# Delta rule: triangle inverses doubled by 64x64 array tiles, with the next pair's levels between this pair's state products

## What is computed

```python
lower = where(strict, einsum('bhntd,bhnsd->bhnts', k_beta, k) * decay, 0)
unit_lower = lower + eye(c)
u = triangular_solve(unit_lower, v_beta)
w = triangular_solve(unit_lower, k_beta * exp(g)[..., None])
attn = where(tri, einsum('bhntd,bhnsd->bhnts', q, k) * decay, 0)
k_tail = k * exp(g_last - g);  q_dec = q * exp(g)
# over the chunks:
v_new = u - w @ state
o = q_dec @ state + attn @ v_new
state = exp(g_last) * state + k_tail.T @ v_new
```

## Time and profile before

| what | value |
|---|---|
| runs | 1901.27, 1905.84, 1907.29 us; median 1905.84 |
| span of the profiled execution | 1897.2 us; of the execution that was profiled the page gives the span alone |
| the median run less that span | 8.6 us |
| the stage: first turn of keys (L1185) to its last output (L1160) | 351.5 to 432.1 us of the span |
| u and w of the four pairs begin at | 365.66, 383.58, 403.35, 422.30 us |
| busiest engine of the whole program | PE, 94% of the span |

### The profile page before, as it was taken

One profiled execution on the slowest core, in us unless ns is written; L12 is line 12 of the kernel. 1 busy time (PEld: TensorE's weight loads), 2 busy tenths in 40 slices (PEclk: granted clock), 3 DMA queues, 4 the chain that ended last, 5 costly groups with the idle time before them and its releaser, 6 DMA issues. The chain is left out here.

```text
span 1897.2 us, 20762 instructions
## 1 busy us (share of the span) xinstructions
PE 1779.8 (94%) x8544; PEld 941.4 (50%) x8544; DVE 697.1 (37%) x1423; ACT 405.5 (21%) x721; POOL 66.4 (3%) x61
## 2 busy tenths in 40 slices
PE   7999999998999998999999999988799999999885
PEld 6785445794555554555543444434355434434342
DVE  3558774453334334444322222212423222222124
ACT  2421332442321222231111111111111111111111
POOL 0000000610000000210000000000000000000000
PEclk9999999999999999999999999999899999999998
DMA  5343332008499992835799999999796999999995
GB/s 211 134 165 135 133 134 49 1 1 356 175 416 412 412 413 106 298 150 219 328 427 429 429 429 429 429 429 427 277 426 276 429 429 428 429 428 430 429 426 220
DMA packets 74531, 583.48 MB, mean 308 GB/s; under 512 B 19323, under 2 KB 21499, under 8 KB 31421
## 3 DMA queue, kind: packets, MB, share of 16 engines
q1 hardware_dynamic: 69677, 580.43, 74.1%
q10 hardware_dynamic: 4752, 1.61, 0.3%
HBM read 578.83 MB, written 3.15 MB: 307 GB/s over the span
## 5 line engine op out<-in xcount | busy, mean ns | idle before, releaser
L1850 PE MATMUL gate_ps_l<-pool,hT 128*64 128x512 f32 x576 | 151.7, 593 | 11.0 <-DMA pool<-in_expert_w_gate 5.7
L1850 PE MATMUL up_ps_l<-pool,hT 128*64 128x512 f32 x576 | 141.7, 595 | 9.2 <-DMA pool<-in_expert_w_up 7.9
L1876 PE MATMUL y_ps_l<-pool,hidden_l 128*64 128x512 f32 x576 | 145.4, 595 | 4.2 <-DMA pool<-in_expert_w_down 2.7
L393 PE MATMUL proj_ps<-pool,hT 128*128 128x512 f32 x320 | 138.3, 592 | 0.0
L2016 DVE SCALAR_TENSOR_TENSOR y_low_l<-y_ps_l,slot_gate_l,y_high_l 128x512 fp32r<-128x512 f32 x64 | 47.9, 751 | 193.5 <-ACT y_high_l L1957 193.5
L385 PE MATMUL proj_ps<-hT,pool 128*128 128x256 f32 x512 | 113.6, 384 | 0.0
L385 PEld LDWEIGHTS proj_ps<-hT,pool 128*128 128x128 f32 x512 | 98.1, 192 | 15.3 <-issue 1.8
L2006 DVE TENSOR_TENSOR hidden_l<-hidden_l,up_ps_l 128x512 f32<-128x512 f32 x32 | 22.0, 688 | 215.3 <-PE up_ps_l L1850 215.3
L393 PEld LDWEIGHTS proj_ps<-pool,hT 128*128 128x128 f32 x320 | 60.8, 190 | 74.4 <-issue 74.1
L1850 PEld LDWEIGHTS gate_ps_l<-pool,hT 128*64 128x64 f32 x576 | 49.8, 137 | 94.7 <-issue 94.7
L1850 PEld LDWEIGHTS up_ps_l<-pool,hT 128*64 128x64 f32 x576 | 45.6, 137 | 85.4 <-issue 85.4
(11 more groups left out here) (534 smaller groups left out, 2896.1 us busy)
## 6 DMA issues: line engine op xcount, KB each, us to landing
pool<-in_expert_w_up SPq DMA_DIRECT2D x36, 2048.0 KB, 30.2
pool<-in_expert_w_down SPq DMA_DIRECT2D x36, 2048.0 KB, 29.7
pool<-in_expert_w_gate SPq DMA_DIRECT2D x36, 2048.0 KB, 31.1
pool<-in_w_in_blocks SPq DMA_DIRECT2D x18, 2048.0 KB, 7.5
gate_room<-in_expert_w_gate SPq DMA_DIRECT2D x14, 2048.0 KB, 24.9
store<-in_expert_w_up SPq DMA_DIRECT2D x14, 2048.0 KB, 22.3
pool<-in_moe_w_gate SPq DMA_DIRECT2D x12, 2048.0 KB, 12.7
pool<-in_moe_w_up SPq DMA_DIRECT2D x12, 2048.0 KB, 12.1
```

Of the source, the lines that this page charges most:

```text
L393: last = mm(pp[:, n % 2, j * W:(j + 1) * W], k.hT[:, c, j * P:(j + 1) * P], wbuf[n % 2][:, c, :], start=(c == 0), stop=(c == KC - 1))
L1850: last = mm(out[e * CAP:(e + 1) * CAP, 0:H], xg(part * r + c)[:, 0, at:at + CAP], ex.weights(i, e, c), start=(part + c == 0), stop=(part = ...
L1876: last = mm(Y[e * CAP:(e + 1) * CAP, n], hidT[:, part * r + c, e * CAP:(e + 1) * CAP], ex.weights(i, e, c)[:, n * W:(n + 1) * W], start=(p ...
```

## The change

- The inner level (32 to 64) is done within the two 64x64 halves of a 128x128 tile: rows 0..63 and 64..127 separately, each a 64x64x64 product. `HALF` names the halves. The upper half's product reads partitions 0..63 and writes 0..63, the lower half's 64..127 and 64..127; calls alternate between them.
- X transposed back is no longer made by turning: the half that the outer level needs is computed directly as `zt` beside `z` (L1248 and L1251 of the new kernel).
- The outer level (64 to 128) computes only the one 64x64 block that is not zero: 4 products for `nL · XT` and 4 for the update. No mask is needed; ACT copies the first result out (`outer_out`) and writes the second straight into XT (`outer_inverse`), which POOL has set to zero once.
- POOL spreads over two block columns instead of four: 256 elements per matrix instead of 512.
- The levels of pair `it + 1` stand between the state products of pair `it`, in new PSUM banks `L[a]` (`gdn_level_ps`); `B` becomes `M1`, `M2` (`gdn_u_ps`, `gdn_w_ps`). Before the loop the levels of pair 0 run alone.
- The scaling of head 1's keys and values moves from ACT (12 instructions) to DVE (3 instructions of 512 elements). ACT's sums of squares move behind the second scaling and write into `k.ob`. q · state is written to `M2` and counted by the same semaphore as w · state; the scaled value goes to a buffer of its own (`qs`).

Only tables and this stage differ. In the constant tables `lev` shrinks from 512 to 128 columns and `same_block` from 128 to 64.

Its core:

```diff
-        X2, XT2, kbg2, ktl2, vb2 = (sb(full, 2) for _ in range(5))
-        V, us, wT = (sb(full) for _ in range(3))
-        B = [[k.ps(f"gdn_ps{a}_{b}", full) for b in range(3)] for a in A]
+        full, square = [P, 2, NJ, P], [P, 2, NJ, CH]
+        kbg2, ktl2, vb2 = (sb(full, 2) for _ in range(3))
+        X2, XT2 = (sb(square, 2) for _ in range(2))
+        XT, us, wT = (sb(full) for _ in range(3))
+        V0 = sb(square)
+        V1, X1 = (sb([P, NJ, CH]) for _ in range(2))
+        S, vn, qs = (sb([P, 2, P]) for _ in range(3))
+        L = [k.ps(f"gdn_level_ps{a}", [P, 2, 2 * NJ * CH]) for a in A]
+        M1, M2 = ([k.ps(f"gdn_{n}_ps{a}", full) for a in A] for n in ("u", "w"))
...
+                for a in A:
+                    nc.gpsimd.memset(XT[a][:], 0.0).then_inc(s_zero[a], 1)
...
+                def outer_out(it):
+                    for a in A:
+                        act.wait_ge(s_v1[a], it + 1)
+                        nc.scalar.activation(V1[a][:], by_tile(L[a][:, 0]), ACT.Copy).then_inc(s_v1s[a], 1)
+
+                def outer_inverse(it):
+                    for a in A:
+                        act.wait_ge(s_z1[a], it + 1)
+                        for d in range(2):
+                            nc.scalar.activation(XT[a][HALF[d], d, :, HALF[1 - d]], by_tile(L[a][HALF[d], 1]),
+                                                 ACT.Copy).then_inc(s_x1[a], 1)
...
+                def inner_inverse(it):
+                    for a in A:
+                        dve.wait_ge(s_z0[a], it + 1)
+                        dve.wait_ge(s_zero[a], 1)
+                        z = by_unit(L[a][:, 1])
+                        for d, r in enumerate(HALF):
+                            tt(X1[a][r], X2[it % 2][a][r, d], by_tile(L[a][r, 0]), ALU.add).then_inc(s_x0[a], 1)
+                            tt(XT[a][r, :, :, r], XT2[it % 2][a][r], z[r], ALU.add).then_inc(s_x0[a], 1)
...
+                def inner(it):
+                    for a, h in heads(it):
+                        pe.wait_ge(s_id[a], 2 * it + 2)
+                        if it:
+                            pe.wait_ge(s_x1[a], 2 * it)
+                        v = by_unit(L[a][:, 0])
+                        for d, j in units():
+                            for r in HALF:
+                                last = mm(v[r, d, j], k.nL[r, h, d, j, r], XT2[it % 2][a][r, d, j],
+                                          start=True, stop=True)
+                        last.then_inc(s_v0[a], 1)
+
+                def inner_update(it):
+                    for a in A:
+                        pe.wait_ge(s_v0s[a], it + 1)
+                        z, zt = by_unit(L[a][:, 1]), by_tile(L[a][:, 0])
+                        X = X2[it % 2][a]
+                        for j in range(NJ):
+                            for d, r in enumerate(HALF):
+                                mm(zt[r, j], V0[a][r, d, j], X[r, d, j], start=True, stop=True)
+                        for d, j in units():
+                            for r in HALF:
+                                last = mm(z[r, d, j], X[r, d, j], V0[a][r, d, j], start=True, stop=True)
+                        last.then_inc(s_z0[a], 1)
+
+                def outer(it):
+                    for a, h in heads(it):
+                        pe.wait_ge(s_x0[a], 4 * it + 4)
+                        v = by_tile(L[a][:, 0])
+                        for j in range(NJ):
+                            for d in range(2):
+                                to, of = HALF[d], HALF[1 - d]
+                                last = mm(v[to, j], k.nL[of, h, d, j, to], XT[a][of, d, j, of], start=True, stop=True)
+                        last.then_inc(s_v1[a], 1)
```

More of the change, by code:

```diff
@@ L81, in tables @@
     )
[L82 to L89, removed]
+    half = (p >> L0) & 1
+    inside, across = np.arange(CH)[None, :] >> L0, np.arange(2 * BS)[None, :] >> L0
+    out["lev"] = np.concatenate([f((half == 0) & (inside == 1)), f((half == 1) & (inside == 0))], 1)
+    out["same_block"] = f(half == across)
     r = np.arange(BS * BS)
@@ L1080, in scaled @@
                 def scaled(it):
[L1081 to L1086, removed]
-                scaled(0)
@@ L1089, in _ @@
[L1089 to L1094, removed]
-                for it in range(NI):
[L1096 to L1102, removed]
+                    act.wait_ge(s_turned[0], it + 1)
@@ new lines, in outer_inverse, with squares @@
+                def outer_inverse(it):
[4 more added lines that the diff above has]
+                                                 ACT.Copy).then_inc(s_x1[a], 1)
+                def squares():
+                    for j in range(NJ):
+                        for h in range(GLA_H):
+                            out = (k.ob[:, j, (h + 1) * GLA_DV:(h + 2) * GLA_DV] if h + 1 < GLA_H
+                                   else squared[:, j])
+                            nc.scalar.activation(out, k.oa[:, j, h * GLA_DV:(h + 1) * GLA_DV], ACT.Square,
+                                                 accum_out=k.mix_var[:, j, h:h + 1]).then_inc(k.s_mix_sq, 1)
@@ L1171, in _ @@
             def _(pe):
-                def each(fn):
-                    for d, j in units():
-                        last = fn(d, j)
-                    return last
                 mm, turn, ident = nc.tensor.matmul, nc.tensor.transpose, k.table("ident")
@@ L1188, in _, with outer_update @@
+                def outer_update(it):
+                    for a in A:
+                        pe.wait_ge(s_v1s[a], it + 1)
+                        z = by_tile(L[a][:, 1])
+                        for j in range(NJ):
+                            for r in HALF:
+                                last = mm(z[r, j], X1[a][r, j], V1[a][r, j], start=True, stop=True)
+                        last.then_inc(s_z1[a], 1)
                 turned(0)
+                inner(0)
+                inner_update(0)
@@ new lines, in _ @@
+                    more = it + 1 < NI
+                    for a in A:
+                        pe.wait_ge(s_nb[a], (12, 3)[a] * (it + 1))
+                        pe.wait_ge(s_x1[a], 2 * it + 2)
+                        if it:
+                            pe.wait_ge(s_hd[a], it)
+                        for d, j in units():
+                            mm(M1[a][:, d, j], XT[a][:, d, j], vb[a][:, d, j], start=True, stop=True)
+                        for d, j in units():
+                            last = mm(M2[a][:, d, j], kbg[a][:, d, j], XT[a][:, d, j], start=True, stop=True)
+                        last.then_inc(s_uw[a], 1)
@@ L1216, in _ @@
+                    if more:
                         turned(it + 1)
+                        inner(it + 1)
                     for a, h in heads(it):
-                        aT = k.aT[:, h]
                         pe.wait_ge(s_uws[a], 2 * it + 2)
                         for d in range(2):
-                            j = first(d)
-                            last = mm(B[a][2][:, 0, d], ktl[a][:, d, j], us[a][:, d, j], start=True, stop=True)
+                            last = mm(M2[a][:, 0, d], ktl[a][:, d, d], us[a][:, d, d], start=True, stop=True)
```

160 lines of the change are left out of this document (86 added, 74 removed).

## The result

The changed kernel takes 1886.89 us (median of 6 executions, 1878.06 to 1890.78), the kernel before 1903.13 beside it (6 executions); the ratio is 0.9919, 95% interval 0.989 to 0.9948. In two later comparisons the same kernel gave 1882.36 against 1900.81 (0.9905) and 1885.43 against 1902.55 (0.9924). The forecast was 1889.4.

The account below looks back on a forecast made before the run. PE was taken to bound the stage. Rounds -14.6, start -3.8 and clock +2.0 sum to -16.4 us off the median 1905.84: 1889.4 us; own range 1884 to 1895, 8 in 10 within 1883 to 1902.

Parts of the forecast that it names:

- The total: Whole kernel: -16.4 us off the median of 1905.84, giving 1889.4 us.
- A small pass at 0.028 us: PE, 64x64 products of the levels: two tiles run side by side, 0.028 us per pass, ends 0.028 and 0.111.
- PE's sum: PE's work per round: 8.9 us full passes, 3.1 small passes, 1.05 changes of shape, together 13.1 us.
- The change of shape: PE switching between full and small tiles: 0.15 us towards small, 0.20 back, three each way, 1.05 us per round.
- The round of 14.0: One pair's u and w to the next's: DVE's tail ends it at 14.0 us; three rounds give -14.6 us.
- The start: Stage start up to the first u and w: these begin at 361.85 instead of 365.66, -3.8 us.
- The clock: PE around the first u and w: 1.2 GHz lasts 3 to 7 us longer, costing +2.0 us.
- The last piece: Stretch after the three rounds, without levels: 9.7 to 9.9 us, no change.
- The first, one tile at a time: Rival 1, PE's small passes: 0.055 us each, rounds 16.5 including 0.35 of waits, kernel 1898.7 us; chance 0.23.
- The second: Rival 2, PE's instruction pace: small passes cost 0.111 us, rounds 22.6, kernel slower at 1918.2 us; chance 0.10.
- 0.062 us per pass: Skill's floor per matmul where firmware decodes, named under rival 2: round 17.4 us, kernel near 1901.
- The third: Rival 3, clock falls inside the rounds through small tiles and gaps: about 3 us per round, kernel 1898; chance 0.12.

Follow-up runs that it names:

- the second profile: The kernel before, unchanged, profiled once more: stage 79.8 us, starting at 357.5 instead of 351.5, rounds 17.92, 19.77 and 18.95 us.
- The split: Two kernels against the kernel before: small tiles with levels ahead of their own u and w, 1899.75 us (1.000); the change's order with full products, 1901.45 us (1.0002).

## Why the prediction held, and where not

**The total** held, 1889.4 against 1886.89, a difference of -16.2 us where -16.4 was summed. That it came so close is luck in part. In the stage the sum promised -16.4, and the profiles show -13.8 (80.6 to 66.8), or -13 to -15 over all pairs of them. The medians moved by 16 to 18 us. The other 2 to 4 us lie outside the stage, within what its neighbours scatter, and no run ties them to the change.

**A small pass at 0.028 us** is right: 32 in 1.08 us with a change of shape, 0.058 when the other half is unused. The two halves write the same PSUM bank (one bank per head holds both levels) from different rows of the array, and no slowdown shows. The Trainium skill, "TensorEngine Tiling (Array Packing)", Restrictions and Gotchas, says that different row tiles cannot access one bank at once. These tiles differ in rows and in columns, and for them the measurement decides: they can.

**PE's sum** of 13.1 us per round came out at 13.65 busy, which counts the last passes' tails. The change of shape cost some 0.35 us there and back (an estimate from the starts of the passes around 405.7 and 406.8), as taken. Neither touches the round, since DVE's tail ends it, as followed.

**The round of 14.0** is the term that was mis-sized: 14.6. The update of head 0 reaches DVE at 8.6 (forecast 8.5), but the eight additions take 2.61 us (409.75 to 412.36), not 2.12. The prediction gave 0.33 us to 256 elements, after an output's addition (L1160) of 0.42 us less a tail; from one of these additions to the next operation it is 0.43 (409.96 to 410.39). The outputs themselves (L1203) still start 0.33 apart, so the price was right for the form that it was read from, and not for additions on 64 partitions into blocks of 64. Which of the two makes them dearer was not tried. Everything behind them is late by that half microsecond. Three rounds gave -12.8 instead of -14.6.

**The start** of -3.8 came out at -3.6 (14.2 to 10.53 us), or -2.8 against the second profile. The clears cost 0.50 us each where 0.6 was taken; the first u and w came 10.5 us after the start, forecast 10.35, and 10.3 in the profile with a start at 0.80.

**The clock**, +2.0, was 2.5, 1.3 and 2.5 us in the first round of the three profiles. It hits u and w, as said, and the levels at the start as well, which the prediction priced at the low clock. In the profiled execution the clock was at 0.50 from 361.0 to 374.7, 13.7 us, against 6.8 us before (353.5 to 360.3, where the prediction read 360.8): 7 us longer, the upper end of the 3 to 7 that it gave.

**The last piece** is 9.91 against 9.80: no change.

**The rivals.** The first, one tile at a time, has its own run: 17.02 per round where 16.5 was worked out, had the halves not run together. The second fell: a small pass is not as dear as a full one, and 0.062 us per pass, the other price named there, doesn't show either (its round of 17.4 adds up to 17.2 with the waits of rival 1). The third didn't come in the change's second and third rounds (1.00 in every profile). It did in the version with the levels apart, in the second and third rounds (0.81 and 0.84), where PE stood idle for 5.0 and 4.6 us; in its first, with 3.7 us idle, the clock was at 1.00.

**What the prediction missed** without harm is how near the other bound lay. It called PE the bound before, with waits only on top of the second round. The split shows that PE's work could have shrunk by 4.2 us a round and given 0.7 at full clock.

## What to carry to other kernels

A stage in which one engine is busy for 94% can still have a chain of waits right behind it; before work is taken off the busy engine, add up the chain alone, and plan to move both. Independent 64x64 products should alternate between two tiles of the array that share neither rows nor columns, and the next step's serial levels belong between this step's products. Then the row order on the engine that ends the round is worth a look: results that the busy engine waits for go ahead of those needed later.

## What was not expected of the hardware

- The order within a group matters less than the use of both halves: eight passes in one half and then eight in the other cost 15.25 us per round against 14.59, while all of them in one tile cost 17.02.
- The unchanged stage ahead ended between 348.2 and 359.3 us in fourteen profiles. In the six profiles whose granted clock in 320 to 350 was 1.00 it ended between 348.2 and 351.5, in the eight with 0.73 to 0.89 between 354.9 and 359.3. PE was busy for 29.3 of these 30 us in the lowest of them. What lets the clock fall there was not tried.
- An addition of 256 elements on 64 partitions, out of PSUM into blocks of 64, starts the next after 0.43 us, one of 128 elements after 0.21.
